# Moving the split activations of eight feed-forward blocks by 4 to 24 bytes, and the rest of the arena by 128

## The chip, the core and the metric

The kernel runs on one core of a Trainium2 chip. The metric is the device time of one execution, in microseconds. The kernel before takes 2555.59 us, the median of two runs (2554.95 and 2556.24).

## The reference, cut to what matters

One sequence of 256 tokens and 1,024 features passes through sixteen blocks; every block normalises its input, projects it with large weight matrices, and adds its result to the residual. Eight of the blocks are feed-forward blocks:

```
def swiglu_ffn(h, w_in, w_out):                 # w_in 1024 x 5632, w_out 2816 x 1024
    gate, up = jnp.split(h @ w_in, 2, axis=-1)
    return (jax.nn.silu(gate) * up) @ w_out
...
x = x + 0.5 * swiglu_ffn(rms_norm(x, g), w_in, w_out)
```

The other blocks are an RWKV mixer, a memory projection, two cross-attentions, a gated MLP over chunks, an HGRN mixer and a dilated attention, with a final norm between. All is float32, and is computed here to more than the accuracy of one pass.

## The kernel before, in words

**Split products.** Every large projection is a product of two float32 numbers, each cut in a high part (rounded to the type float32r, which TensorE takes in one pass) and a low part (the remainder). Three matmuls are added up: weights high x activations high, weights high x activations low, weights low x activations high. The activations are the *moving* operand: 256 columns (the tokens), 1,024 bytes in each partition. The weights are the loaded operand: 128 columns, 512 bytes in each partition. So each of the three matmuls comes with a weight load of its own.

**Weights.** One slab is 128 rows of output features: 8 chunks of 128x128 for a projection out of 1,024 features, 11 for half of one out of 2,816. SyncE's queue brings slabs into `raw`, a ring of four; ScalarE writes `hi` from it (`act_hi`, L348), VectorE writes `lo` (`dve_lo`, L356), and TensorE reads both.

**Activations.** `Hh` and `Hl` (8 KB in each partition, 8 chunks of 1,024 bytes) hold the scaled input of a projection, written by `prep` (ScalarE L599, VectorE L611). `Ah` and `Al` (22 KB each) hold the activation between the two projections of a feed-forward block, written by `FeedForward.act` (L795) and `FeedForward.dve` (L837). All eight feed-forward blocks use the same `Hh`, `Hl`, `Ah`, `Al`. `Kh` and `Kl` hold the input of the dilated attention's keys and values.

**A feed-forward block.** Input stage: 44 slabs x 8 chunks x 3 = 1,056 matmuls on `Hh`/`Hl`. Output stage: 16 slabs x 11 chunks x 3 = 528 on `Ah`/`Al`. The first two slabs of an input stage are unrolled (L468 to L470), then the sum for the norm is made by one float32 matmul on the masks (L699), then come the slabs of a loop (L487, L491, L492). In some iterations ahead of the loop, one of the three matmuls, in its fourth chunk, is cut in two pieces of 192 and 64 columns with the same weights; below it is called the **parted pair** (`pe_parted`, L396). L410, L414 and L415 are the same three matmuls in `pe_slab`, for mixers.

**Where things lie.** `self.arena` starts at a byte that is 64 more than a multiple of 256. `at` places every named array of the blocks in it at an offset, and all the large offsets are multiples of 1 KB. `hi` and `lo`, and each chunk in them, start 128 bytes past a multiple of 512. So each moving operand of a split product starts at 320 modulo 512 and each weight chunk at 128 modulo 512: a distance of 192 (modulo 256) that is the same for all of them in this kernel. The order of the work on each engine is written out in the code, and none of it depends on addresses.

Of the kernel before, what the change touches and what calls it, by code (L numbers as in the profile page):

```python
# [30 lines left out]
P = 128  # L31
T = 256
# [158 lines left out]

UNSPLIT = ("mix_norm0",)
# [27 lines left out]
class Resources:  # L220


    def __init__(self, nc, ctx, io, counts):
# [23 lines left out]
        self.arena = sb("arena", [P, (self.room - 128) // 4])  # L247
        self.limit = self.room - 128
# [18 lines left out]
        self.Ah = self.at("Ah", self.A0, [P, FC, T], F32R)  # L267
        self.Al = self.at("Al", self.A0 + 22 * KB, [P, FC, T], F32R)
# [39 lines left out]
    def at(self, name, offset, shape, dt=F32):  # L308

        size = 4 * int(np.prod(shape[1:]))  # L310
        assert offset + size <= self.limit, (name, offset, size, self.limit)
        return self.nc.alloc_sbuf_tensor_at(name, shape, dt, offset=self.base + offset)

# [13 lines left out]
class Shared:  # L327
# [222 lines left out]
    def pe_first_stage(self, pe, st, pair=False, norm=None):  # L550

        self.split_n["pe"] += NC
        self.pe_stage_h(pe, st, lambda: (norm or self.norm)(pe, "pe"), pair=pair)

    def pe_entry_stage(self, pe, st):

        k = self.k
        self.split_n["pe"] += NC
        self.pe_stage_h(pe, st, entry=True)

    def pe_stage_h(self, pe, st, after_first=None, rest=False, pair=False, entry=False):

        k, n = self.k, self.split_n["pe"] - NC
        self.pe_stage(pe, st, lambda kg, kc: (k.Hh[:, kc, :], k.Hl[:, kc, :]),
# [23 lines left out]
    def prep(self, eng, e, src, gain, c, split=True, square=True, wait=None):  # L588

        k, twice = self.k, gain == "final_norm"  # L590
        ns, nq = self.split_n[e] + c, self.square_n[e] + c
        scale = k.both_gains[:, c:c + 1] if twice else k.v1(gain, c)
        if e == "act":
            if wait:
                wait(c)
            if split:
                if twice:
                    eng.wait_ge(k.both_ready, 2)
                eng.activation(k.Hh[:, c, :], src[:, c, :], ACT.Copy, scale=scale).then_inc(k.h_hi, 1)  # L599
# [8 lines left out]
        else:  # L608
            if split:
                eng.wait_ge(k.h_hi, ns + 1)  # L610
                eng.scalar_tensor_tensor(k.Hl[:, c, :], src[:, c, :], scale,  # L611
                                         k.Hh[:, c, :].bitcast(F32), ALU.mult, ALU.subtract).then_inc(k.h_lo, 1)
# [141 lines left out]
class FeedForward:  # L754


    def __init__(self, sh, name, order, nxt, keys_next=False, keys_now=False, normed_twice=False):
# [4 lines left out]
        self.st_in, self.st_out = sh.stage[f"ffn_in{name[3]}"], sh.stage[f"ffn_out{name[3]}"]  # L762

    def pe(self, pe):
        sh, k = self.sh, self.k
        if self.n == 0:
            pe.wait_ge(k.x_loaded[0], 16)
            sh.pe_keep_awake(pe, 5, k.X[:, 0, :P], k.X[:, 1, :])
            sh.pe_entry_stage(pe, self.st_in)
        else:  # L770
            sh.pe_first_stage(pe, self.st_in, norm=self.norm)
        done = 2 + FC * self.n
        sh.pe_stage(pe, self.st_out,
                    lambda kg, kc: (k.Ah[:, kg * WIDE + kc, :], k.Al[:, kg * WIDE + kc, :]),
# [2523 lines left out]
```

## Time and profile before

| | us |
|---|---|
| median of two runs | 2555.59 |
| the profiled execution, its own time | 2556.5 |
| its span in the profile | 2554.7 |
| busy time of TensorE's matmuls | 2489.3 |
| busy time of VectorE | 1744.9 |
| busy time of ScalarE | 1316.9 |

The profiled execution's time is 1.8 us above its span; the rest lies outside the profiled instructions. "PE" is TensorE's matmul side and "PEld" its weight load. A matmul's own duration in the profile (277 ns) is the time from its start to the end of its drain, and those of neighbours overlap; what a stream of them costs is the **distance between two starts**. Over a long window without a gap, it is the window's length plus one duration (0.277 us, since matmuls that only reach into the window are counted too), divided by the number of matmuls.

### The profile page before, as it was taken

The page shows a single profiled execution, that of the slowest core. Times are in us where ns is not written, and L with a number is a line of the kernel's source. Part 1 is how long each engine was busy: PE and PEld are TensorE (multiplying, and loading weights), DVE is VectorE, ACT ScalarE, POOL GpSimd, SP SyncE. Part 2 cuts the span into 40 slices and gives each one's busy share as a digit, 9 for nine tenths or more (in the row PEclk, how much of TensorE's full clock was granted, in tenths as well). Part 3 has the DMA queues.
Part 4 walks back from the last instruction along what each step waited for, and adds up shares of the span by engine and source line. Part 5 has one row for each costly group of instructions (what it writes and reads, how often), then busy time and mean ns, then how long its engine had stood idle before and what let it go on. Part 6 is the DMA issues. An engine that isn't in the chain of part 4 may idle for free.

```text
span 2554.7 us, 60487 instructions
## 1 busy us (share of the span) xinstructions
PE 2489.3 (97%) x23329; PEld 2423.8 (95%) x23329; DVE 1744.9 (68%) x2871; ACT 1316.9 (52%) x1997; POOL 79.0 (3%) x122
## 2 busy tenths in 40 slices
PE   8998998999999999999999999899999999999999
PEld 8997977989999999989999999899999999999999
DVE  6757677567766757767766767967667666666774
ACT  5534444455545546555545547455455455555552
POOL 0000442000000000000000000000000000000000
PEclk9999999999999999999999999999999999999999
DMA  6663301435655656445655655246656665553664
GB/s 203 218 211 125 100 12 44 149 126 181 208 185 188 212 202 185 153 136 182 207 181 188 211 176 190 75 126 201 203 173 201 200 188 153 157 157 111 195 210 136
DMA packets 119840, 425.14 MB, mean 166 GB/s; under 512 B 16673, under 2 KB 24564, under 8 KB 119412
## 3 DMA queue, kind: packets, MB, share of 16 engines
q1 hardware_dynamic: 111616, 411.65, 49.7%
q10 hardware_dynamic: 8052, 11.04, 2.3%
q8 instruction: 127, 2.08, 0.3%
q14 instruction: 45, 0.37, 0.0%
HBM read 421.51 MB, written 1.12 MB: 165 GB/s over the span
## 4 chain that ended last, share of the span: by engine, by line
PE 87%; DVE 5%; ACT 3%; issue 2%; POOL 1%; SPq 0%; DMA 0%; ACTq 0%; DVEq 0%; POOLq 0%
PE bank L492 20%; PE bank L487 20%; PE bank L491 20%; PE bank L410 5%; PE bank L415 4%; PE bank L414 4%; ACT hi L348 1%; PE bank L2410 1%; DVE lo L356 1%; PE bank L468 1%; PE bank L470 1%; PE bank L469 1%; PE bank L1812 1%; PE bank L1785 1%; PE bank L1797 1%
## 5 line engine op out<-in xcount | busy, mean ns | idle before, releaser
L356 DVE TENSOR_TENSOR lo<-raw,hi 128x1024 fp32r<-128x1024 f32 (+1 forms) x728 | 935.3, 1293 | 381.0 <-ACT hi L348 379.2
L348 ACT ACTIVATE hi<-raw 128x1024 fp32r<-128x1024 f32 (+1 forms) x728 | 782.2, 1106 | 292.9 <-PE bank L415 168.1
L487 PE MATMUL bank<-Hh,hi 128*128 128x256 f32 x3024 | 836.3, 277 | 3.1 <-DVE lo L356 2.0
L492 PE MATMUL bank<-Hh,lo 128*128 128x256 f32 x3024 | 837.4, 277 | 0.0
L491 PE MATMUL bank<-Hl,hi 128*128 128x256 f32 x3004 | 830.1, 276 | 0.0
L487 PEld LDWEIGHTS bank<-Hh,hi 128*128 128x128 f32 x3024 | 567.9, 188 | 4.3 <-DVE lo L356 4.0
L492 PEld LDWEIGHTS bank<-Hh,lo 128*128 128x128 f32 x3024 | 568.1, 188 | 0.0
L491 PEld LDWEIGHTS bank<-Hl,hi 128*128 128x128 f32 x3004 | 564.3, 188 | 0.0
L487 PE MATMUL bank<-Ah,hi 128*128 128x256 f32 x1408 | 389.7, 277 | 1.9 <-DVE lo L356 1.9
L492 PE MATMUL bank<-Ah,lo 128*128 128x256 f32 x1408 | 390.1, 277 | 0.0
L491 PE MATMUL bank<-Al,hi 128*128 128x256 f32 x1400 | 387.2, 277 | 0.0
L487 PEld LDWEIGHTS bank<-Ah,hi 128*128 128x128 f32 x1408 | 265.1, 188 | 2.1 <-DVE lo L356 2.1
L492 PEld LDWEIGHTS bank<-Ah,lo 128*128 128x128 f32 x1408 | 265.1, 188 | 0.0
L491 PEld LDWEIGHTS bank<-Al,hi 128*128 128x128 f32 x1400 | 263.6, 188 | 0.0
L790 ACT ACTIVATE sgate<-gate 128x256 f32<-128x256 f32 x176 | 73.6, 418 | 228.7 <-DVE gate L823 228.7
L795 ACT ACTIVATE Ah<-act 128x256 f32 (+1 forms) x176 | 73.7, 419 | 215.2 <-DVE act L832 215.2
L410 PE MATMUL bank<-Hh,hi 128*128 128x256 f32 x560 | 160.0, 286 | 0.0
L677 DVE SCALAR_TENSOR_TENSOR X<-bank,X 128x256 f32<-128x256 f32 x112 | 47.5, 424 | 163.0 <-PE bank L492 155.1
L415 PE MATMUL bank<-Hh,lo 128*128 128x256 f32 x560 | 155.9, 278 | 0.0
L414 PE MATMUL bank<-Hl,hi 128*128 128x256 f32 x559 | 155.4, 278 | 0.0
L599 ACT ACTIVATE Hh<-X,vec 128x256 fp32r<-128x256 f32 x96 | 47.8, 504 | 196.6 <-DVE X L677 193.8
L410 PE MATMUL bank<-Kh,hi 128*128 128x256 f32 x384 | 111.6, 291 | 0.0
(445 smaller groups left out, 4042.3 us busy)
## 6 DMA issues: line engine op xcount, KB each, us to landing
raw<-in_w SPq DMA_DIRECT2D x600, 512.0 KB, 3.7
raw<-in_w SPq DMA_DIRECT2D x128, 704.0 KB, 4.9
dB<-dil_bias ACTq DMA_DIRECT2D x16, 384.0 KB, 10.4
X<-in_x SPq DMA_DIRECT2D x2, 512.0 KB, 5.9
mem_x<-in_mem ACTq DMA_DIRECT2D x2, 512.0 KB, 4.4
gWS<-in_ws ACTq DMA_DIRECT2D x1, 1024.0 KB
gBS<-in_bs ACTq DMA_DIRECT2D x1, 1024.0 KB
out_x<-X SPq DMA_DIRECT2D x4, 256.0 KB, 2.6
```

Of the source, the lines that this page charges most:

```text
L348: act.activation(k.hi[:, q, :w], k.raw[:, q, :w], ACT.Copy).then_inc(k.hi_ready, 1)
L356: dve.tensor_tensor(k.lo[:, q, :w], k.raw[:, q, :w], k.hi[:, q, :w].bitcast(F32), ALU.subtract).then_inc(k.lo_ready, 1)
L410: pe.matmul(out, wh, xh, start=first and kc == 0, stop=False)
L414: pe.matmul(out, wh, xl, start=False, stop=False)
L415: mm = pe.matmul(out, wl, xh, start=False, stop=last)
L487: pe.matmul(out, wh, xh, start=first, stop=False)
L491: pe.matmul(out, wh, xl, start=False, stop=False)
L492: mm = pe.matmul(out, wl, xh, start=False, stop=last)
L599: eng.activation(k.Hh[:, c, :], src[:, c, :], ACT.Copy, scale=scale).then_inc(k.h_hi, 1)
L677: dve.scalar_tensor_tensor(k.X[:, c, :], k.bank[s % RING][:, :T], coef, k.X[:, c, :], ALU.mult, ALU.add).then_inc(k.banks_freed, st.per_tile)
L790: act.activation(k.sgate[:, j, :], k.gate[:, j, :], ACT.Silu).then_inc(k.silu_done, 1)
L795: act.activation(k.Ah[:, bass.ds(m, 1), :].rearrange("p a t -> p (a t)"), k.act32[:, j, :], ACT.Copy).then_inc(k.ah_ready, 1)
```

## The change

Eight pairs of homes for `Hh`/`Hl` and eight for `Ah`/`Al` take the place of one each; the names are `Hh0` ... `Hl7`, `Ah0` ... `Al7`, and they overlap in memory as before. `skewed` allocates one at an offset that need only be a multiple of 4. The loop bodies, the semaphores and the order are the same: each engine has the same instructions in the same order, only start addresses differ. Besides, `at` moves every array at or above 16 KB by 128 bytes and every one at or above 84 KB by 256.

The distance from a weight chunk to the moving operand, modulo 256, was 192 for all. Now it is, by feed-forward block:

| block | 0 | 1 | 2 | 3 | 4 | 5 | 6 | 7 |
|---|---|---|---|---|---|---|---|---|
| input stage (`H`) | 208 | 200 | 196 | 176 | 184 | 216 | 204 | 188 |
| output stage (`A`) | 192 | 112 | 144 | 208 | 176 | 200 | 80 | 184 |

The mixers' own `Hh`/`Hl` (the key `None`) stay at 192. Their other moving operands (`Kh`/`Kl`, the inputs of the RWKV projections, the inputs of the output projections) go from 192 to 64.

```diff
@@ -189,6 +189,9 @@
            "ffn4": "norm_gain00", "hgrn": "norm_gain01", "ffn5": "norm_gain02",
            "ffn6": "norm_gain10", "dil": "norm_gain11", "ffn7": "norm_gain12"}
 
+PHASE_H = ((16, 16), (8, 8), (4, 4), (240, 240), (248, 248), (24, 24), (12, 12), (252, 252))
+PHASE_A = ((128, 128), (48, 48), (80, 80), (144, 144), (112, 112), (136, 136), (16, 16), (120, 120))
+
 UNSPLIT = ("mix_norm0",)
 
 
@@ -244,8 +247,8 @@
         self.sel = sb("sel", [P, NC * 16])
         self.base = -(-nc.sbuf_base // 64) * 64
         self.room = nc.sbuf_usable_end - self.base
-        self.arena = sb("arena", [P, (self.room - 128) // 4])
-        self.limit = self.room - 128
+        self.arena = sb("arena", [P, (self.room - 64) // 4])
+        self.limit = self.room
 
 
         self.Hh = self.at("Hh", 0, [P, NC, T], F32R)
@@ -264,8 +267,13 @@
         self.FSUM = self.at("FSUM", 88 * KB, [P, T])
         self.FSTD = self.at("FSTD", 89 * KB, [P, T])
         self.A0 = 40 * KB
-        self.Ah = self.at("Ah", self.A0, [P, FC, T], F32R)
-        self.Al = self.at("Al", self.A0 + 22 * KB, [P, FC, T], F32R)
+        self.H = {None: (self.Hh, self.Hl)}
+        self.A = []
+        for n, (h, a) in enumerate(zip(PHASE_H, PHASE_A)):
+            self.H[GAIN_OF[f"ffn{n}"]] = tuple(self.skewed(f"H{x}{n}", 8 * KB * j + h[j], NC)
+                                               for j, x in enumerate("hl"))
+            self.A.append(tuple(self.skewed(f"A{x}{n}", self.A0 + 22 * KB * j + a[j], FC)
+                                for j, x in enumerate("hl")))
 
         self.bank = [ctx.enter_context(nc.psum_tensor(f"bank{b}", [P, 512], F32)) for b in range(8)]
 
@@ -308,8 +316,15 @@
     def at(self, name, offset, shape, dt=F32):
 
         size = 4 * int(np.prod(shape[1:]))
+        offset += P * ((offset >= 16 * KB) + (offset >= 84 * KB))
         assert offset + size <= self.limit, (name, offset, size, self.limit)
         return self.nc.alloc_sbuf_tensor_at(name, shape, dt, offset=self.base + offset)
+
+    def skewed(self, name, offset, chunks):
+
+        skew = offset % 32 // 4
+        t = self.at(name, offset - 4 * skew, [P, chunks * T + skew], F32R)
+        return t[:, skew:].rearrange("p (c t) -> p c t", c=chunks)
 
     def mask(self, name, n=1):
 
@@ -547,21 +562,22 @@
             with pe.Fori(min(2, st.iters - 1), st.iters) as i:
                 body(i)
 
-    def pe_first_stage(self, pe, st, pair=False, norm=None):
+    def pe_first_stage(self, pe, st, pair=False, norm=None, gain=None):
 
         self.split_n["pe"] += NC
-        self.pe_stage_h(pe, st, lambda: (norm or self.norm)(pe, "pe"), pair=pair)
-
-    def pe_entry_stage(self, pe, st):
+        self.pe_stage_h(pe, st, lambda: (norm or self.norm)(pe, "pe"), pair=pair, gain=gain)
+
+    def pe_entry_stage(self, pe, st, gain):
 
         k = self.k
         self.split_n["pe"] += NC
-        self.pe_stage_h(pe, st, entry=True)
-
-    def pe_stage_h(self, pe, st, after_first=None, rest=False, pair=False, entry=False):
+        self.pe_stage_h(pe, st, entry=True, gain=gain)
+
+    def pe_stage_h(self, pe, st, after_first=None, rest=False, pair=False, entry=False, gain=None):
 
         k, n = self.k, self.split_n["pe"] - NC
-        self.pe_stage(pe, st, lambda kg, kc: (k.Hh[:, kc, :], k.Hl[:, kc, :]),
+        Hh, Hl = k.H[gain]
+        self.pe_stage(pe, st, lambda kg, kc: (Hh[:, kc, :], Hl[:, kc, :]),
                       lambda kg, kc: pe.wait_ge(k.h_lo, n + kc + 1), after_first=after_first, rest=rest, pair=pair, entry=entry)
 
     def dve_project(self, dve, st, dest, scaled=True, before=None, between=None):
@@ -588,6 +604,7 @@
     def prep(self, eng, e, src, gain, c, split=True, square=True, wait=None):
 
         k, twice = self.k, gain == "final_norm"
+        Hh, Hl = k.H[GAIN_OF['ffn4'] if gain == 'final_norm' else gain if gain in k.H else None]
         ns, nq = self.split_n[e] + c, self.square_n[e] + c
         scale = k.both_gains[:, c:c + 1] if twice else k.v1(gain, c)
         if e == "act":
@@ -596,7 +613,7 @@
             if split:
                 if twice:
                     eng.wait_ge(k.both_ready, 2)
-                eng.activation(k.Hh[:, c, :], src[:, c, :], ACT.Copy, scale=scale).then_inc(k.h_hi, 1)
+                eng.activation(Hh[:, c, :], src[:, c, :], ACT.Copy, scale=scale).then_inc(k.h_hi, 1)
             if square:
                 if nq >= 2:
                     eng.wait_ge(k.sq_added, nq - 1)
@@ -608,8 +625,8 @@
         else:
             if split:
                 eng.wait_ge(k.h_hi, ns + 1)
-                eng.scalar_tensor_tensor(k.Hl[:, c, :], src[:, c, :], scale,
-                                         k.Hh[:, c, :].bitcast(F32), ALU.mult, ALU.subtract).then_inc(k.h_lo, 1)
+                eng.scalar_tensor_tensor(Hl[:, c, :], src[:, c, :], scale,
+                                         Hh[:, c, :].bitcast(F32), ALU.mult, ALU.subtract).then_inc(k.h_lo, 1)
             if square:
                 eng.wait_ge(k.sq_ready, nq + 1)
                 if c == 0:
@@ -760,18 +777,20 @@
         self.normed_twice = normed_twice
         self.keys_next, self.keys_now = keys_next, keys_now
         self.st_in, self.st_out = sh.stage[f"ffn_in{name[3]}"], sh.stage[f"ffn_out{name[3]}"]
+        self.gain = GAIN_OF[name]
+        self.Ah, self.Al = self.k.A[order]
 
     def pe(self, pe):
         sh, k = self.sh, self.k
         if self.n == 0:
             pe.wait_ge(k.x_loaded[0], 16)
             sh.pe_keep_awake(pe, 5, k.X[:, 0, :P], k.X[:, 1, :])
-            sh.pe_entry_stage(pe, self.st_in)
+            sh.pe_entry_stage(pe, self.st_in, self.gain)
         else:
-            sh.pe_first_stage(pe, self.st_in, norm=self.norm)
+            sh.pe_first_stage(pe, self.st_in, norm=self.norm, gain=self.gain)
         done = 2 + FC * self.n
         sh.pe_stage(pe, self.st_out,
-                    lambda kg, kc: (k.Ah[:, kg * WIDE + kc, :], k.Al[:, kg * WIDE + kc, :]),
+                    lambda kg, kc: (self.Ah[:, kg * WIDE + kc, :], self.Al[:, kg * WIDE + kc, :]),
                     lambda kg, kc: pe.wait_ge(k.al_ready, done + WIDE * kg + kc + 1))
 
     def act(self, act):
@@ -792,7 +811,7 @@
                     sh.act_hi(act, s + RING, 2 * j, ahead, turn)
                     sh.act_hi(act, s + 1 + RING, 2 * j + 1, ahead, turn)
                 act.wait_ge(k.a_ready, g + 3)
-                act.activation(k.Ah[:, bass.ds(m, 1), :].rearrange("p a t -> p (a t)"), k.act32[:, j, :],
+                act.activation(self.Ah[:, bass.ds(m, 1), :].rearrange("p a t -> p (a t)"), k.act32[:, j, :],
                                ACT.Copy).then_inc(k.ah_ready, 1)
         if self.n == 0:
             body(0, st.width, split_before=True)
@@ -834,8 +853,8 @@
                     sh.dve_lo(dve, s + 1 + RING, 2 * j + 1, ahead)
                 dve.wait_ge(k.ah_ready, g + 1)
                 dve.wait_ge(k.a_ready, g + 3)
-                dve.tensor_tensor(k.Al[:, bass.ds(m, 1), :].rearrange("p a t -> p (a t)"), k.act32[:, j, :],
-                                  k.Ah[:, bass.ds(m, 1), :].rearrange("p a t -> p (a t)").bitcast(F32),
+                dve.tensor_tensor(self.Al[:, bass.ds(m, 1), :].rearrange("p a t -> p (a t)"), k.act32[:, j, :],
+                                  self.Ah[:, bass.ds(m, 1), :].rearrange("p a t -> p (a t)").bitcast(F32),
                                   ALU.subtract).then_inc(k.al_ready, 1)
         if self.n == 0:
             body(0, st.width, split_before=True)
```

## Rows read from the trace of the kernel before

**Rows 1.** The page: busy time by engine, and the granted clock in 40 slices.
```profile
PE 2489.3 (97%) x23329; PEld 2423.8 (95%) x23329; DVE 1744.9 (68%) x2871; ACT 1316.9 (52%) x1997; POOL 79.0 (3%) x122
...
PEclk9999999999999999999999999999999999999999
```

**Rows 2.** The page: the chain that ended last, by engine and line.
```profile
PE 87%; DVE 5%; ACT 3%; issue 2%; POOL 1%; SPq 0%; DMA 0%; ACTq 0%; DVEq 0%; POOLq 0%
```

**Rows 3.** The page: costliest groups, as busy us, mean ns | idle before, releaser.
```profile
L487 PE MATMUL bank<-Hh,hi 128*128 128x256 f32 x3024 | 836.3, 277 | 3.1 <-DVE lo L356 2.0
...
L487 PE MATMUL bank<-Ah,hi 128*128 128x256 f32 x1408 | 389.7, 277 | 1.9 <-DVE lo L356 1.9
...
L487 PEld LDWEIGHTS bank<-Ah,hi 128*128 128x128 f32 x1408 | 265.1, 188 | 2.1 <-DVE lo L356 2.1
...
L410 PE MATMUL bank<-Kh,hi 128*128 128x256 f32 x384 | 111.6, 291 | 0.0
```

**Rows 4.** Windows, TensorE: stretch, length, busy us (matmuls), granted clock, DMA share, GB/s.
```profile
620.00:700.00 80.00, 80.00 (x708) 1.00 0.64 203
720.00:760.00 40.00, 40.00 (x355) 1.00 0.57 186
2400.00:2480.00 80.00, 80.00 (x708) 1.00 0.63 204
500.00:508.00 8.00, 8.00 (x70) 1.00 0.44 138
510.00:520.00 10.00, 10.00 (x91) 1.00 0.58 179
1140.50:1148.50 8.00, 8.00 (x70) 1.00 0.20 66
1152.00:1160.00 8.00, 8.00 (x73) 1.00 0.63 197
1052.00:1072.00 20.00, 20.00 (x172) 1.00 0.51 159
1075.00:1095.00 20.00, 20.00 (x172) 1.00 0.57 182
```

**Rows 5.** Timeline, TensorE, second feed-forward input stage, its first parted pair: start, us.
```profile
595.82 0.28 PE L492 MATMUL bank<-Hh,lo 128*128 128x256 f32 x1
...
596.65 0.28 PE L487 MATMUL bank<-Hh,hi 128*128 128x256 f32 x1
596.76 0.30 PE L396 MATMUL bank<-Hl,hi 128*128 128x192 f32 x2
...
598.03 0.28 PE L492 MATMUL bank<-Hh,lo 128*128 128x256 f32 x1
...
600.19 0.28 PE L487 MATMUL bank<-Hh,hi 128*128 128x256 f32 x1
```

**Rows 6.** Timeline, TensorE, the parted pair of the gated MLP's output projection.
```profile
1072.17 0.31 PE L396 MATMUL bank<-gGl,hi 128*128 128x192 f32 x2
```

**Rows 7.** Timeline, TensorE: eight matmuls of 128 columns, and six transposes, a load each.
```profile
1018.04 1.06 PE L1102 MATMUL bank<-gWS,gVT 128*128 128x128 f32 x8
...
2096.46 0.82 PE L1754 MATMUL bank<-masks,dVF 128*128 128x128 f32 x6
```

**Rows 8.** By line: VectorE and ScalarE, count, duration ns least/median/most.
```profile
L2752 DVE TENSOR_TENSOR rDX<-rH x8: 418/422/423, 204.1 to 214.0; 128x255 f32<-128x255 f32 x8
L837 DVE TENSOR_TENSOR Al<-act,Ah x176: 416/419/425, 27.6 to 2494.6; 128x256 f32 x156, 128x256 fp32r<-128x256 f32 x20
L2635 ACT ACTIVATE rPPX<-rCS x8: 400/416/418, 270.8 to 391.3; 128x256 f32<-128x256 f32 x8
L795 ACT ACTIVATE Ah<-act x176: 417/419/422, 27.2 to 2493.2; 128x256 f32 x158, 128x256 fp32r<-128x256 f32 x18
```

**Rows 9.** Waits of the whole trace, TensorE: us in total, times, longest.
```profile
PE bank L487 <- DVE lo L356: 6.8, 6, 1.9
```

## The prediction

> **What bounds the kernel now.** I read the page's busy times first. TensorE's matmuls are busy for 2489.3 of 2554.7 us, at a granted clock of 0.9 or more in every slice [rows 1], and the chain of work that ended last is TensorE for 87% [rows 2]. VectorE (1744.9 us) and ScalarE (1316.9 us) have room. Then the waits: the loop's matmuls waited 6.8 us for `lo`, over the whole trace [rows 9]. So nothing is short but TensorE itself, and a change of addresses can matter only if it changes how fast a matmul follows another.
>
> That is not seen in a matmul's duration (277 ns, drain included [rows 3]) but in the distance between starts, which I take from windows without a gap: (length + 0.277 us) / count. In two windows of feed-forward input stages it is 80.277/708 = 0.1134 us, in one of an output stage 40.277/355 = 0.1135 us [rows 4]. The gated MLP's output projection, with operands at the same distance, same shapes and the same granted clock of 1.00, takes 20.277/172 = 0.1179 us [rows 4]. So there are **two levels**, 0.1134 and 0.118, and the address distance alone does not choose between them, since it is 192 for both.
>
> What chooses is where the stream of loads stands against the stream of moving columns, and that is kept until something disturbs it. The second feed-forward input stage comes out of the norm at the slow level (seven steps from 595.82 to 596.65, 0.1186 each at the rows' resolution of 0.01), meets the parted pair at 596.76, and goes on at 2.16 us for 19 steps, 0.1137 [rows 5]. RWKV's output projection goes from 8.277/70 = 0.1182 to 10.277/91 = 0.1129 over its pair, the second cross-attention's from 0.1182 to 8.277/73 = 0.1134 [rows 4]. The gated MLP's has its pair too, at 1072.17 [rows 6], and has 172 matmuls in 20 us on both sides of it [rows 4]: there the pair frees nothing.
>
> **What the change removes, adds and moves.** It adds no instruction and no wait, and it moves no instruction on any queue. The DMAs into `raw` and the weights stay where they were. What changes is the start address of moving operands: 15 of the 16 feed-forward streams (the first block's output stage keeps 192), which are 8 x 1,056 + 7 x 528 = 12,144 matmuls, and 3,072 of the mixers (keys and values 3 x 384 [rows 3], the other inputs of RWKV's and the output projections). The counts of the code agree with the trace, 1,408 = 8 x 176 of each kind in the output stages [rows 3].
>
> *Writers.* ScalarE and VectorE now write at starts off 16 bytes. The trace has such work: a subtraction reads and writes one element off, 255 elements in 422 ns, against 419 for 256 aligned ones, and an activation writes one element off in 416 ns, against 419 [rows 8]. I take nothing, and if there were something, VectorE and ScalarE have the idle time named above.
>
> *A shorter distance between matmuls.* Unknown, so bounded. The nearest rows with a load each are eight matmuls of 128 columns, (1.06 - 0.28)/7 = 0.111 us, and six transposes, (0.82 - 0.27)/5 = 0.110 [rows 7]. Their moving and loaded operands are another pair of distances, and 128 columns leave the load less company. Best case: all 12,144 go to 0.110, 12,144 x 0.0034 = 41 us, and the mixers' 3,072 another 10. It is a far bound: it asks that every one of seven to fifteen distances be better than the present one.
>
> *A longer distance.* The level that the trace shows costs 0.0045 us a matmul: 4.8 us for an input stage, 2.4 for an output stage, 54.6 us for all 12,144. For the mixers' 3,072 it is 13.8 us at most, of which the gated MLP's 384 pay 1.7 already and could give it back. Farther up no row goes; as an estimate I let one more step of the same size be possible.
>
> *What I take.* Both levels stay, and a stream stays slow where its parted pair no longer frees it, because the pair's two pieces (192 and 64 columns) hit the loads at another point. How often? Of the eleven pairs whose streams I can sort, eight in feed-forward input stages (rows 5 show one, the others repeat it) and three in output projections of mixers, one fails. Of the three in mixers alone it is one. That is 15/11 = 1.4 to 15/3 = 5 of the 15 streams; I take 3. A mean stream is 810 matmuls, 3.6 us: **+11 us**, from +5 to +18. The mixers I take at nothing, because some are slow today and could gain as others lose.
>
> *Two rules beside it.* Starts off 16 bytes: in the rows, a longer fetch of the moving operand would be hidden, because the load paces the pair (matmuls of 128 columns follow each other at 0.111, of 256 at 0.1134 [rows 4, 7]). The Trainium skill's page "SBUF — State Buffer" (Specifications) says that lines are of 16 bytes and that each crossing to a new one costs something. If it is one line of 65 instead of 64 in the eight streams off 16 bytes, one sixty-fourth of 0.1134 for 7,392 matmuls, that is 13 us as an estimate, and the sum would be 2580 with my own term. No run here shows it.
>
> **The rivals.**
>
> *Distance doesn't matter at all.* The levels come from timing alone and the pairs go on freeing what they freed: 2556, within 3. For it: the same distance gives both levels in rows 4, and the chunks' places beyond 512 bytes vary with no trace of it in the windows. Against it: a stream that keeps a level for tens of microseconds is locked by something that it shares with the loads, and addresses are the plainest candidate. The Trainium skill's page "TensorE: Matmul & The Clock Gate" (Step-by-step: what each phase is for) says that the moving operand and the load have independent read ports, so a load takes no bandwidth from a running matmul; by that rule this rival is what happens. The two levels of rows 4 speak against the rule's being whole.
>
> *Better distances.* Some blocks lie between 0.1134 and 0.111: half of the 0.0024 for all 12,144 is 15 us, so 2541, down to 2526 if all reach 0.111. For it: fast is still 6% over 256 columns at 2.4 GHz (0.1067 us), so there is something to win. Against it: the 0.111 rows say that the load alone holds most of that.
>
> *Collisions, slower than before.* New distances put loads and columns on the same part of the memory at the same time, and nothing frees them: all 15 streams at 0.118, 2556 + 54.6 = 2611; with eight of them a step worse, 12,144 x 0.0045 and 6,336 x 0.0045 are 83 us, so 2639. It crosses 2% (51 us) from 14 slow streams, or from ten where four are a step worse. For it: the gated MLP's pair shows that a stream can fail to be freed. Against it: eight different distances in each group would all have to be bad.
>
> *A kernel faster by over 2%* needs 51 us, which is more than the far bound of 41 us plus 10 for the mixers; it is possible only if the load itself gets faster.
>
> **How the numbers follow.** The profiled execution took 2556.5 us, 0.9 above the median of 2555.6; I add to the median. Forecast 2556 + 11 = 2567, chance 0.37, own range 2560 to 2574. No effect 0.22. Better distances 0.23, of which 0.02 beyond 2%. Collisions 0.18: 0.11 over 2607 and 0.07 between 2580 and 2607. The range leaves out the last part of the better distances below 2530 (about 0.05) and of the collisions above 2611 (about 0.08): 2530 to 2611. A measurement of this kernel spreads over 1.3 us, far less than the 2% (51 us) that the chances are asked for. Faster by over 2%: 0.02. Slower by over 2%: 0.11. Within: 0.87.
>
> **What would show it.** In windows inside each feed-forward stage, the count gives the distance between starts. My forecast wants 0.1134 in most, and 0.118 in two to five streams, from their parted pair on. The first block's output stage is a control: its distance is 192 still. If every window shows 0.113, distance doesn't matter. Values between, such as 0.112 or 0.115, would say that distance sets levels of its own, and then my two-level picture is wrong; if so, odd multiples of 4 should stand apart from multiples of 16 if lines matter. `Ah`, `Al`, `Hh` and `Hl` writes writes of `A` should stay within 10 ns of their 419. If TensorE's waits for `lo` grow past some microseconds, or if the mixers' 3,072 move by more than 10 us together, the sum above has left something out.

## The result, and the profile after

The changed kernel takes 2622.77 us (median of two runs, 2622.24 and 2623.30) against 2555.59: a ratio of 1.0267, interval 1.0244 to 1.0290, so it is slower. The span grew from 2554.7 to 2621.5 us.

Its busy times, which answer to [rows 1]:

```profile
PE 2556.9 (98%) x23329; PEld 2491.6 (95%) x23329; DVE 1758.9 (67%) x2871; ACT 1327.0 (51%) x1997; POOL 79.1 (3%) x122
```

TensorE's matmuls are busy for 67.6 us more, with the same count; the other engines' busy time moved by 14 us or less. The bound is the same and the work is the same: a matmul follows the one before it more slowly. The matmuls' own durations, which answer to [rows 3], hide most of that, 282 ns for 277 (mean ns, behind the busy time):

```profile
L502 PE MATMUL bank<-Hh,hi 128*128 128x256 f32 x3024 | 852.8, 282 | 3.4 <-DVE lo L371 2.4
```

So I go by windows, as in [rows 4]: stretch, length, busy us (matmuls), granted clock, DMA share, GB/s. Below, the spacing is the distance between two starts. Here are one window inside the input stage and one inside the output stage of each block, 0 to 7, in order of time:

```profile
core 0: us, PE busy (x), PEclk, DMA share, GB/s
40.00:130.00 90.00, 90.00 (x759) 1.00 0.62 202
150.00:195.00 45.00, 45.00 (x399) 1.00 0.55 181
620.00:700.00 80.00, 80.00 (x669) 1.00 0.57 190
720.00:760.00 40.00, 40.00 (x355) 1.00 0.54 175
790.00:880.00 90.00, 90.00 (x742) 1.00 0.56 187
910.00:950.00 40.00, 40.00 (x343) 1.00 0.52 171
1200.00:1290.00 90.00, 90.00 (x757) 1.00 0.58 193
1320.00:1360.00 40.00, 40.00 (x338) 1.00 0.53 171
1390.00:1480.00 90.00, 90.00 (x752) 1.00 0.58 191
1510.00:1550.00 40.00, 40.00 (x338) 1.00 0.53 172
1750.00:1840.00 90.00, 90.00 (x749) 1.00 0.57 187
1870.00:1910.00 40.00, 40.00 (x336) 1.00 0.51 167
1940.00:2030.00 90.00, 90.00 (x766) 1.00 0.58 194
2060.00:2100.00 40.00, 40.00 (x336) 1.00 0.50 172
2440.00:2540.00 100.00, 100.00 (x845) 1.00 0.60 196
2560.00:2610.00 50.00, 50.00 (x419) 1.00 0.37 122
```

The spacing is (length + 0.28)/count. For the input stages it is 0.1190, 0.1200, 0.1217, 0.1193, 0.1201, 0.1205, 0.1179 and 0.1187 us; for the output stages 0.1135, 0.1135, 0.1174, 0.1192, 0.1192, 0.1199, 0.1199 and 0.1200. The granted clock is 1.00 in all. Only the first output stage (192, the control) and the second (112) are as before.

The excess over 0.1134, times 1,056 for an input stage, is 52.6 us over the eight, and times 528 for an output stage, 18.6 us: 71 us, against 67 that the span grew.

What came back lies ahead of block 1. Its input stage starts at 585.4 us against 586.9 before, though block 0's input stage alone has an excess of 6 us; from there to the end the changed kernel falls 68 us behind. Part of it is the granted clock. The kernel before waited 1.92 us for `lo` at the border between block 0's two stages (first row, from its timeline), and behind that wait it stood at the lower of TensorE's two levels (1.2 GHz) for a while. The changed kernel did neither. The second and third row are the same window before and after:

```profile
137.17 0.36 PE L487 MATMUL bank<-Ah,hi 128*128 128x256 f32 x1 [1.92 <-DVE lo L356]
136.00:141.00 5.00, 3.83 (x21) 0.69 0.91 310
136.00:141.00 5.00, 5.00 (x45) 1.00 0.97 360
```

The mixers became slower too. Five of their output projections (RWKV, both cross-attentions, HGRN, dilated attention) had a mean spacing of 113.5 to 115.6 ns before and have 117.8 now, which is 3 us; RWKV's other inputs add 1 us. The memory projection, whose operand kept distance 192, was at its slow level before (117.4 ns) and mostly at the fast one now (114.0), 1 us less; so a level can differ where no address of the stream did. (Of the dilated attention's two inputs only the high half went to distance 64. The low half lies above 84 KB, moved by 256 bytes and kept 192.)

The writers did not feel their new starts; these rows answer to [rows 8], least/median/most ns, 418 each where 419 stood:

```profile
L856 DVE TENSOR_TENSOR Al<-act,Ah x176: 415/418/427, 26.4 to 2556.9; 128x256 f32 x156, 128x256 fp32r<-128x256 f32 x20
...
L814 ACT ACTIVATE Ah<-act x176: 417/418/422, 25.9 to 2555.5; 128x256 f32 x158, 128x256 fp32r<-128x256 f32 x18
```

### The profile page after: what moved, and what is told of

The parts are those of the page before. It is cut to its first block, busy times and chain, and to the rows that moved or that the text cites. A ratio compares the mean times of both kernels' runs of the same rounds, so it can differ in the third digit from the quotient of the medians.

```text
span 2621.5 us, 60487 instructions
## 1 busy us (share of the span) xinstructions
PE 2556.9 (98%) x23329; PEld 2491.6 (95%) x23329; DVE 1758.9 (67%) x2871; ACT 1327.0 (51%) x1997; POOL 79.1 (3%) x122
## 4 chain that ended last, share of the span: by engine, by line
PE 86%; DVE 4%; ACT 2%; issue 1%; POOL 1%; ACTq 0%; DMA 0%; DVEq 0%; POOLq 0%
PE bank L502 20%; PE bank L507 20%; PE bank L506 20%; PE bank L425 5%; PE bank L430 4%; PE bank L429 4%; PE bank L2429 1%; ACT hi L363 1%; PE bank L483 1%; PE bank L484 1%; PE bank L485 1%; PE bank L1831 1%; DVE lo L371 1%; PE bank L1804 1%; PE bank L1350 1%
## 5 line engine op out<-in xcount | busy, mean ns | idle before, releaser
L363 ACT ACTIVATE hi<-raw 128x1024 fp32r<-128x1024 f32 (+1 forms) x728 | 792.5, 1107 | 386.4 <-PE bank L507 190.5
L502 PE MATMUL bank<-Hh,hi 128*128 128x256 f32 x3024 | 852.8, 282 | 3.4 <-DVE lo L371 2.4
L507 PE MATMUL bank<-Hh,lo 128*128 128x256 f32 x3024 | 851.4, 282 | 0.0
L506 PE MATMUL bank<-Hl,hi 128*128 128x256 f32 x3004 | 846.5, 282 | 0.0
L506 PEld LDWEIGHTS bank<-Hl,hi 128*128 128x128 f32 x3004 | 571.3, 190 | 0.0
L502 PE MATMUL bank<-Ah,hi 128*128 128x256 f32 x1408 | 395.1, 281 | 1.4 <-DVE Al L856 1.4
L506 PE MATMUL bank<-Al,hi 128*128 128x256 f32 x1400 | 393.1, 281 | 0.0
L425 PE MATMUL bank<-Hh,hi 128*128 128x256 f32 x560 | 161.0, 287 | 0.0
L430 PE MATMUL bank<-Hh,lo 128*128 128x256 f32 x560 | 156.7, 280 | 0.0
L429 PE MATMUL bank<-Hl,hi 128*128 128x256 f32 x559 | 156.3, 280 | 0.0
```

The source lines that it names most:

```text
L363: act.activation(k.hi[:, q, :w], k.raw[:, q, :w], ACT.Copy).then_inc(k.hi_ready, 1)
L425: pe.matmul(out, wh, xh, start=first and kc == 0, stop=False)
L429: pe.matmul(out, wh, xl, start=False, stop=False)
L430: mm = pe.matmul(out, wl, xh, start=False, stop=last)
L502: pe.matmul(out, wh, xh, start=first, stop=False)
L506: pe.matmul(out, wh, xl, start=False, stop=False)
```

## The experiments

Each is a change to the changed kernel or to the kernel before, and each ratio is against executions of the kernel before made beside it. Rows are windows of TensorE with the columns as above, unless said otherwise. A mean over a whole stage, given in ns, leaves out steps under 105 and over 140 ns: waits and the pieces of parted pairs. All distances are modulo 256, unless said otherwise. The slow level of 192 is 0.1177, its fast level 0.1134.

### Only the shift of the other arrays

```diff
-PHASE_H = ((16, 16), (8, 8), ...
+PHASE_H = ((0, 0), (0, 0), ...      # eight times
-PHASE_A = ((128, 128), (48, 48), ...
+PHASE_A = ((128, 128), (128, 128), ...
```

> The changed kernel with every feed-forward home back at distance 192 (H offset 0, A offset 128), so that only the shift of the other arrays by 128 and 256 bytes is left; their distance is 64, as in the changed kernel. Theory 1 (the loss of 67 us lies in the feed-forward streams, because of their distances): 2551 to 2560 us, all sixteen streams at 0.1134. Theory 2 (the shift of the rest costs, for instance because the split operands now share something with it): clearly above 2560, with mixers' streams or the feed-forward ones above 0.115.

The median is 2561.45 us against 2554.23, ratio 1.0026 (1.0011 to 1.0041). The loss is gone but for 7 us. In the profiled execution one block stands out. The rows are the input stage of block 5, the one of block 6, and the first part of block 6's output stage:

```profile
1700.00:1800.00 100.00, 100.00 (x883) 1.00 0.59 190
1900.00:1980.00 80.00, 80.00 (x681) 1.00 0.59 193
2005.00:2030.00 25.00, 25.00 (x216) 1.00 0.51 169
508.00:518.00 10.00, 10.00 (x87) 1.00 0.53 175
```

The first three are 0.1136, 0.1179 and 0.1170: block 6 stayed at the slow level of 192 until some way into its output stage (the means of its stages are 117.6 and 115.4 ns), some 5 us lost. The last row is RWKV's output projection behind its parted pair, now at distance 64: 0.1182, where [rows 4] had 0.1129. All five output projections named above are at 117.8 ns here as well, 3 us, so theory 2 holds for a few microseconds: the shift is not free. The mean granted clock of the nine executions was 0.994, against 0.996 beside them, which also costs something. Theory 1 holds for the rest of the 67 us. How the last 7 us divide among these three isn't shown.

### Only the input stages

```diff
-PHASE_A = ((128, 128), (48, 48), ...
+PHASE_A = ((128, 128), (128, 128), ...      # eight times; PHASE_H as in the changed kernel
```

> The changed kernel with the eight output stages (A) back at distance 192 and the input stages (H) at their eight new distances. Theory 1 (each stream has the spacing of its own distance, whatever came before it): the input stages as in the changed kernel, 0.118 to 0.122, and the output stages at 0.1134; time before + 51 us less some 2 us of the mixers, about 2604. Rival (a stream inherits its level from the one before it, since the lock is kept until something disturbs it): output stages after a slow input stage stay near 0.118 or above, and the time is near 2615.

The median is 2612.45 us, ratio 1.0231 (1.0210 to 1.0251). The rows are block 1's input stage, then the output stages of blocks 1 and 2:

```profile
620.00:700.00 80.00, 80.00 (x669) 1.00 0.57 188
730.00:770.00 40.00, 40.00 (x349) 1.00 0.53 172
920.00:960.00 40.00, 40.00 (x355) 1.00 0.51 171
```

The input stage has its 0.1200 again. Block 2's output stage comes behind the slowest input stage (0.1217) and is at 0.1135; block 1's is at 0.1154 over its window, since it starts at the slow level of 192 and is freed on the way. So a stream's spacing comes from its own placement; what it can inherit is which of its own levels it starts on. That is worth 2, 1 and 1 us in blocks 0, 1 and 6 here (means 117.3, 115.4 and 115.4 ns). The time is 8 us above my sum. The other 4 us fit the mixers: the sum took 2 us off for them, and their five output projections are at 117.8 ns here too, 3 us more than before.

### The same distances in other blocks

```diff
+PHASE_H = ((252, 252), (16, 16), (12, 12), (24, 24), (240, 240), (8, 8), (4, 4), (248, 248))
+PHASE_A = ((120, 120), (16, 16), (136, 136), (112, 112), (144, 144), (80, 80), (48, 48), (128, 128))
```

> The changed kernel's sixteen distances given to other blocks (input stages 188, 208, 204, 216, 176, 200, 196, 184; output stages 184, 80, 200, 176, 208, 144, 112, 192 for blocks 0 to 7). Theory 1 (the distance sets the spacing): output stages with 192 and 112 at 0.1134, the one with 144 near 0.1177, the five others 0.119 to 0.120, each as it was in another block; time within 5 us of 2623. Rival (the block sets it: its place in the program, the state in which the stream starts): the fast output stages are still those of blocks 0 and 1.

The median is 2626.08 us, ratio 1.0284 (1.0262 to 1.0306). The rows are block 2's input stage (now 204) and output stage (200), and block 6's output stage (112):

```profile
800.00:900.00 100.00, 100.00 (x851) 1.00 0.60 195
930.00:970.00 40.00, 40.00 (x336) 1.00 0.53 167
2080.00:2115.00 35.00, 35.00 (x311) 1.00 0.56 185
```

0.1178, 0.1199, 0.1134. Here are the means of the steps between starts over whole stages, in ns, each distance in its first block and in its new one:

| | 176 | 184 | 188 | 196 | 200 | 204 | 208 | 216 |
|---|---|---|---|---|---|---|---|---|
| input, changed kernel | 119.24 | 120.01 | 118.60 | 121.66 | 120.04 | 117.78 | 118.85 | 120.70 |
| input, this one | 119.25 | 120.00 | 118.57 | 121.67 | 120.06 | 117.82 | 119.15 | 120.70 |

Of the output stages, seven agree within 0.1 (112: 113.49 and 113.52); only 144 differs, 117.75 and 118.67. So with the weights at their old place the distance sets the spacing, to within 0.3 ns in 15 of 16 stages, and the block doesn't.

### The kernel before without its parted pairs

```diff
-                    if parted and q == RING - 1 and kc == 3:
+                    if False:
```

and the same in `pe_slab`.

> The kernel before, with the parted pair made one whole matmul everywhere. Every distance is 192. If two levels exist at 192 and the pair is what frees a stream, the input stages stay at 0.1177 from the norm on: 8 x 1,056 x 0.0044 = 37 us, and up to 19 more if the output stages inherit it: 2590 to 2612. If the distance alone sets the level and the pair did nothing: 2554 to 2557.

The median is 2578.44 us, ratio 1.0097 (1.0077 to 1.0118), below the range that I gave (2590 to 2612). Block 1's two stages, then block 2's input stage:

```profile
600.00:700.00 100.00, 100.00 (x852) 1.00 0.62 200
720.00:760.00 40.00, 40.00 (x342) 1.00 0.55 173
790.00:880.00 90.00, 90.00 (x797) 1.00 0.62 202
```

Block 1 stays at 0.1177 and 0.1178, block 2 at 0.1133. Four of the eight blocks stay slow, four come out fast by themselves. So two levels at distance 192 are shown, and the pairs are worth 24 us. The slow ones (blocks 1, 4, 6 and 7) turn slow at the norm or at the loop's next iteration and stay so to the end of their output stage.

### Thirty-two streams at other distances

Two runs with sixteen streams each; only the tables change.

```diff
+PHASE_H = (distance - 192) % 256, twice, for each block
+PHASE_A = (distance - 64) % 256, twice, for each block
```

> The changed kernel with sixteen other distances, most of them multiples of 32: input stages 0, 224, 64, 128, 160, 96, 240, 112 and output stages 0, 32, 64, 96, 128, 160, 112, 224 for blocks 0 to 7. Theory A (what counts is the distance modulo 64, the usual 192 being 0): 0, 64 and 128 have the fast level 0.1134 or the slow one 0.1177, all others 0.117 to 0.121. Theory B (modulo 128, since 112 was fast and 176 not): 0 with 128, 96 with 224, 32 with 160 alike, 112 with 240 alike and fast, 64 as 192. Theory C (no period below 256): sixteen unrelated values. A value below 0.1133 anywhere would say that the usual distance is not the best.

> The changed kernel with sixteen more distances: input stages 120, 16, 48, 144, 108, 116, 32, 104 and output stages 16, 48, 240, 120, 116, 108, 104, 72. If only multiples of 16 can be fast, 104, 108, 116, 120 and 72 lie at 0.118 to 0.121 although 112 between them is fast in an output stage (0.1135); if a neighbourhood of 112 is good, some of them lie below 0.117. 144 should be near 0.118 in an input stage as in an output stage, and 48 near the 0.1193 of 176 if the period is 128.

One execution each, 2609.85 and 2633.34 us. The rows are the first one's output stage of block 0 (distance 0) and input stage of block 7 (112):

```profile
150.00:190.00 40.00, 40.00 (x335) 1.00 0.57 184
2425.00:2525.00 100.00, 100.00 (x883) 1.00 0.60 194
```

0.1202 and 0.1136. Here are all distances measured so far with the weights at their old place, mean spacing of whole stages in ns; where two stand, both were seen:

| distance | ns | distance | ns | distance | ns |
|---|---|---|---|---|---|
| 0 | 120.0 | 104 | 120.1 | 176 | 119.2 |
| 16 | 118.5 | 108 | 120.0 | 184 | 120.0 |
| 32 | 116.7 | **112** | **113.5** | 188 | 118.6 |
| 48 | 118.3 | 116 | 121.8 | **192** | **113.4**, 117.8 |
| 64 | **113.4** (parts of mixers), 117.8 | 120 | 120.1, 121.8 | 196 | 121.7 |
| 72 | 121.7 | 128 | 118.7 | 200 | 120.0 |
| 80 | 120.0 | 144 | 116.9 to 118.7 | 204 | 117.8 |
| 96 | 120.0 | 160 | 117.5, 117.9 | 208 | 118.9 to 119.2 |
| | | 224, 240 | 118.3, 117.1 | 216 | 120.7 |

Input and output stages mostly agree (32: 116.68 and 116.67). The exceptions are 120 (121.84 and 120.10), 160 (117.51 and 117.94) and 144. Theories A and B fall: 0 and 128 have neither level of 192 and differ from each other, and 48 differs from 176.

Distance 64 is less simple. Both of its feed-forward stages here are at 117.8, which is also the slow level of 192. But the mixers' output projections lie at 64 in these runs, and they are not always slow. The rows are RWKV's in the second run, ahead of its parted pair (at 517.99 us) and behind it, and HGRN's two halves in the run with one half of the activations off (below):

```profile
509.50:517.50 8.00, 8.00 (x73) 1.00 0.43 135
521.00:529.00 8.00, 8.00 (x70) 1.00 0.52 184
1695.00:1705.00 10.00, 10.00 (x91) 1.00 0.01 2
1709.00:1717.00 8.00, 8.00 (x70) 1.00 0.75 248
```

That is 0.1134, 0.1183, 0.1130 and 0.1183: distance 64 has both levels as well, and the pair, which leads streams at 192 out of the slow level, here stood where a fast stream turned slow.

Nothing is below 113.3. Of the whole feed-forward stages only those at 112 and 192 reach it, and four bytes off either cost 5 to 8 ns. Leaving those out, the multiples of 16 have 116.7 to 120.0 as stages and the others 117.8 to 121.8, so a start off 16 bytes is not the cause by itself.

### Distance or alignment: the weights moved by 16 bytes

`hi` and `lo` start 16 bytes later, at 144 modulo 256; some moving operands follow, and `at` has no shift:

```diff
+        n = RING * WIDE * P
+        split = sb("split", [P, 2 * n + 64], F32R)
+        self.hi = split[:, 4:4 + n].rearrange("p (r w) -> p r w", r=RING)
+        self.lo = split[:, 4 + n:4 + 2 * n].rearrange("p (r w) -> p r w", r=RING)
+PHASE_H = 16 in blocks 0, 3, 4, 5, 7, else 0; PHASE_A = 16, in block 6 0
-        offset += P * ((offset >= 16 * KB) + (offset >= 84 * KB))
```

> The high and low weights start 16 bytes later, and so do the moving operands of input stages 0, 3, 4, 5, 7 and of all output stages but that of block 6: distance 192 again, but all starts off 64 bytes. The operands that were not moved (input stages 1, 2, 6, output stage 6, and the mixers) have distance 176. If the distance counts: the moved ones 0.1134 (or the slow level of 0.1177 where a pair misses), the others 0.119 as at 176 in the changed kernel, and the mixers slow as well: 2554 plus 3 x 5.9 + 3.1 us for those, and up to 5,800 x 0.0055 = 32 us for the mixers: 2575 to 2610. If alignment of the moving operand itself counts: the other way round, the unmoved ones at 0.1134 and the moved ones at 0.119, about 2615.

The median is 2591.16 us, ratio 1.0125 (1.0069 to 1.0182). The rows are block 1's input stage (operands unmoved, 176), block 3's (moved, 192) and RWKV's output projection (unmoved, 176):

```profile
620.00:700.00 80.00, 80.00 (x676) 1.00 0.60 193
1200.00:1300.00 100.00, 100.00 (x885) 1.00 0.64 206
503.00:522.00 19.00, 19.00 (x163) 1.00 0.52 168
```

That is 0.1188 with the moving operand where it always was, and 0.1133 with both starts moved by 16 bytes. It is the distance and not the place of the moving operand. The mixers, for which nothing of their own was changed, became slow (0.1183 in the third row).

### Distance 112 everywhere

This is the kernel before with the weights 80 bytes up; every moving operand keeps its place modulo 256. It ran once with its pairs and once without.

```diff
+        self.hi = split[:, 20:20 + n]...      # and lo, as above; the arena moves up by 256
```

> The kernel before with the high and low weights moved 80 bytes up, so that every split matmul of the program has distance 112; the moving operands stay where they are, and the parted pairs stay. 112 was the only distance beside 192 that came out at 0.1135. If it is as good as 192 and no better: all feed-forward streams 0.1134 to 0.1136, time within 3 us of before. If 112 has no slow level, the mixers' streams that sit at 0.1177 in the kernel before (the gated MLP's output 384, the memory projection 312, parts of the others, some 2,000 matmuls) get 0.0044 shorter as well: 9 us less, 2546. If it has a slow level that other streams fall into: over 2560.

> The same, distance 112 everywhere, with the parted pair made one whole matmul. If 112 has one level only: as the run with pairs, within 3 us, and every feed-forward stream at 0.1135. If it has two levels as 192 has: some streams at 0.1177 or above, and 20 to 57 us more.

The medians are 2650.26 us, ratio 1.0370 (1.0352 to 1.0389), and 2644.35 us, ratio 1.0352 (1.0331 to 1.0372). The first meets only its last alternative, over 2560, and no stream is fast; the second is 6 us below the first, where I had the same or 20 to 57 more. Block 1's stages, with pairs:

```profile
620.00:700.00 80.00, 80.00 (x670) 1.00 0.58 190
730.00:775.00 45.00, 45.00 (x378) 1.00 0.50 166
```

Both are 0.1198: distance 112 is slow here. Whole stages have 118.5 to 120.0 ns with pairs and 118.3 to 120.0 without. So the distance alone is not the whole of it, and two more runs ask what else is.

### Two runs on what 112 lacks

> As the run with the weights 80 bytes up, but the moving operands of input stages 0, 3, 4, 5, 7 and of all output stages but that of block 6 go up by 80 as well: their distance is 192 again, the others' stays 112. If the distance alone counts: the moved ones 0.1134, and the others as in the run with the weights alone 80 bytes up, 0.1185 to 0.120. If the place of the weights themselves makes them slow (a chunk then starts 208 bytes past a multiple of 256, instead of 128): the moved ones are slow too, 0.118 or more.

```diff
+        self.hi = split[:, 20:20 + n]...      # and lo
+PHASE_H = 80 in blocks 0, 3, 4, 5, 7, else 0; PHASE_A = 80, in block 6 0
-        offset += P * ((offset >= 16 * KB) + (offset >= 84 * KB))
```

The median is 2599.27 us, ratio 1.0166 (1.0140 to 1.0193). Block 2's input stage (unmoved, 112) and block 3's (moved, 192):

```profile
800.00:900.00 100.00, 100.00 (x836) 1.00 0.59 196
1200.00:1300.00 100.00, 100.00 (x884) 1.00 0.64 205
```

That is 0.1200 and 0.1134: the weights' place does no harm to 192.

> Weights at their old place, distance 112 modulo 256 in all but three input stages and two output stages, in two kinds: modulo 512 it is 368, as in all streams so far that were fast at 112 (input stages 4 and 5, output stages 1, 3 and 5), or 112, as in the slow streams of the run with the weights 80 bytes up (input stages 0 and 3, output stages 0, 2, 4 and 7). If the period is 512: the first kind 0.1135, the second 0.118 to 0.120. If the period is 256, all are 0.1135, and it is the weights' own place that made the difference. Input stages 1 and 2 have 320 (64 modulo 256), input stage 7 has 368, input stage 6 192, output stage 6 has 448 (192 modulo 256).

```diff
+PHASE_H = 432, 128, 128, 432, 176, 432, 0, 176
+PHASE_A = 304, 48, 304, 48, 304, 48, 128, 304
```

One execution, 2567.56 us. Output stages of block 0 (112 modulo 512) and block 1 (368):

```profile
140.00:190.00 50.00, 50.00 (x441) 1.00 0.56 187
720.00:760.00 40.00, 40.00 (x355) 1.00 0.57 185
```

That is 0.1140 (its pairs included) and 0.1135; all twelve streams at 112 of both kinds were at 113.4 to 113.6. (Block 5's input stage is of the first of these kinds, not of the second, as my expectation has it.) Block 6, at 192, stayed slow again, as in the run with the shift alone: 117.6 and 115.4. So the period of the moving side is 256, and with the weights at 128 modulo 256 the distance 112 is fast, with them at 208 it isn't. Why 192 is fast at three places of the weights and 112 at one of two stays open.

### One half of the activations off

```diff
+PHASE_H = ((0, 8), (0, 8), (0, 16), (8, 256), (0, 0), (16, 256), (0, 0), (8, 256))
+PHASE_A = ((128, 136), (128, 144), (128, 128), (136, 384), (128, 128), (144, 384), (128, 128), (136, 384))
```

> The changed kernel with only one half of the activations off 192. Low half off (one of three matmuls): input stages 0 and 1 and output stage 0 at 200, input stage 2 and output stage 1 at 208. High half off (two of three matmuls): input stage 3, input stage 7, output stages 3 and 7 at 200, input stage 5 and output stage 5 at 208. All else 192. If each matmul pays for its own distance: low half at 200 gives (2 x 113.4 + 120.0)/3 = 115.6 ns, high half (113.4 + 2 x 120.0)/3 = 117.8; at 208 115.3 and 117.3. If the spacing is a lock of the whole stream: values away from these, 113.4 or 120 among them.

The median is 2599.58 us, ratio 1.0172 (1.0148 to 1.0196). Block 1's input stage (low half at 200) and block 3's (high half at 200):

```profile
610.00:700.00 90.00, 90.00 (x766) 1.00 0.59 195
1200.00:1300.00 100.00, 100.00 (x833) 1.00 0.58 192
```

That is 0.1179 and 0.1204; whole stages have 117.8 and 120.4 ns, and at 208 117.1 and 118.5. Paying matmul by matmul would have given 115.6 and 117.8. One operand in three at 200 adds 4.4 ns to 113.4 and two in three add 7.0, where all three add 6.6. So the price is not paid matmul by matmul; the spacing belongs to the sequence of starts as a whole. The 117.8 alone would prove less, since it is also the slow level of 192; 117.1, 118.5 and 120.4 are no level of 192.

### More pairs

```diff
-                    if parted and q == RING - 1 and kc == 3:
+                    if q == RING - 1 and kc == 3:
```

> The kernel before with a parted pair in the fourth slab of every iteration of every projection, instead of the first iterations alone; all distances 192. A pair takes no longer than the matmul that it replaces. If a pair frees a slow stream and a fast one finds back in a few matmuls: no stream stays slow for long, the mixers' streams at 0.1177 end early, 2545 to 2553, and the spread between runs gets smaller. If a pair also throws fast streams into the slow level: above 2560. The gated MLP's output projection, which its one pair didn't free, tells whether one more does.

The median is 2572.53 us, ratio 1.0059 (1.0042 to 1.0076): slower than before. The gated MLP's output projection does come down, to 113.5 ns on average from 117.8, and block 6 ends at 114.0. But I had a price wrong. A fast stream's timeline around a pair (start, us):

```profile
625.83 0.30 PE L396 MATMUL bank<-Hl,hi 128*128 128x192 f32 x2
...
626.17 0.28 PE L487 MATMUL bank<-Hh,hi 128*128 128x256 f32 x1
```

From the pair's start (625.83, x2) over one more matmul to the next (626.17) are 0.34 us, where two matmuls take 0.23: a pair costs a load more, 0.11 us. The page has 147 matmuls more than before (23,476), one for each added pair: some 17 us, more than the slow streams had to give. With this price the run without pairs adds up: its four slow blocks cost 26 us by their means, and 33 pairs less (x23296 on its page) give 4 back, which makes some 23 of the 24 us.

## Why the prediction was wrong

**What bounds the kernel** held: TensorE alone. Its waits for `lo` did not grow (6.8 us before, 5.2 after), and a change of the spacing of its matmuls went into the time nearly whole (71 us of windows, 67 of time).

**The writers** at nothing held (418 ns). **The shift of the mixers' arrays** at nothing was a term too low by some 4 us, within its bound of 13.8: the reason given, that some could gain as others lose, did not come true, since at distance 64 none gained.

**The step that failed** is "Both levels stay, and a stream stays slow where its parted pair no longer frees it", with its 3 streams of 15. I had seen that one distance gives two levels, and concluded that "the address distance alone does not choose". In the trace before, every split product has distance 192, so no row could say what another distance does; from one value of a quantity nothing follows on its effect. The runs showed that ten of the eleven new distances have only spacings of 0.117 to 0.122, the same in any block within 0.3 ns but for 144 (116.9 to 118.7), and that the pair doesn't lead out of them: 14 streams of 15 were slow, not 3. What the step describes, a pair that frees nothing, did happen at distance 192, in block 6 of two other runs, for 5 us. That its cause is where the loads stand against the moving columns was argued in the prediction and is not shown by any run. The rival "collisions" had what the runs show, new distances that are slower and that nothing frees, and its bracket of 2611 to 2639 holds the time; I gave it 0.18 and let the range end at its lower edge. Its reason, loads and columns on the same part of the memory at the same time, was argued; no run shows it. The rival's price was one level's 0.0045 for 12,144 matmuls, 54.6 us; the measured mean is 71/12,144 = 0.0058.

**Two readings of the rows** were off besides. Of the eight pairs in input stages, two freed nothing, because the stream was fast already: block 5's went at 0.1131 over the 13 steps ahead of its pair, and block 0's had turned fast long before its own (113.3 ns over the 60 steps ahead of it). The run without pairs has four fast blocks. So how often a pair matters was overrated.

```profile
1701.80 0.28 PE L487 MATMUL bank<-Hh,hi 128*128 128x256 f32 x1
...
1703.27 0.28 PE L491 MATMUL bank<-Hl,hi 128*128 128x256 f32 x1
...
1703.61 0.30 PE L396 MATMUL bank<-Hl,hi 128*128 128x192 f32 x2
```

And the matmuls of [rows 7] work on float32 arrays, the split products on float32r. That the load paces both does not follow from them.

**The bound on a gain** held: none of the 27 distances measured had a stage below 0.1133.

**The two rules.** By the Trainium skill's page "TensorE: Matmul & The Clock Gate" (Step-by-step: what each phase is for), the two read ports are independent and a load takes nothing from a running matmul. As the prediction used it, no distance should then matter; the traces give 0.1134 and 0.1200 for the same instructions at other addresses, so the measurement decides against that rule for this case. The Trainium skill's page "SBUF — State Buffer" (Specifications) says that each crossing to a new 16-byte line costs something. The prediction took from it that starts off 16 bytes are slower: 204 has 117.8 and 80 has 120.0, so it doesn't order them. No run changes the start against the lines and keeps the distance, so what a crossing costs here isn't shown.

## What to carry to other kernels

Where a stream of matmuls has a weight load each and the windows show a spacing above the columns' own time, the place of the moving operand against the weights is a tuning parameter worth up to 7% of that spacing, and moving any buffer, even one pad, can change it unseen. Keep the distance of a fast kernel fixed when its arrays move; the distance alone was not enough for 112, so measure the spacing in windows after each change of layout. When all rows share one value of a quantity, give the unknown its full room, however flat it looks.

## What the runs showed of the hardware

- The spacing of 128x128 loads with 256 moving columns, at a granted clock of 1.00, is 113.3 to 121.8 ns in whole stages, and changing nothing but the two start addresses moves it over that range; at distance 192 it was 113.4 with the weights at 128, 144 and 208 modulo 256.
- Some placements have more than one level: 113.4 and 117.8 at distances 192 and 64, and 118.3 and 120.0 at 112 with the weights at 208 modulo 256. Distance 120 gave 121.8 in an input stage and 120.1 in an output stage.
- It does not depend on the block beyond 0.3 ns in 15 of the 16 stages whose distances were exchanged (144 differs by 0.9), and at distance 112 it did not depend on 256 bytes more for the moving operand.
- A stream can keep its level for a whole stage and take it over the border between stages: without pairs, four blocks stayed at 117.8 ns from the norm, or the loop's next iteration, to their end.
- The kernel before spread from 2549.91 to 2563.32 us over twelve executions. Over all 34 that were made beside the experiments, the time goes with the mean granted clock: the eight at 0.994 or less took 2557.2 to 2564.9 us (mean 2561.2), the thirteen at 0.996 or more 2549.9 to 2559.5 (mean 2553.6). One block at the slow level would be 7 us, which would fit too, but that was seen in two variants of the changed kernel (block 6) and not in the one profile of the kernel before.
